# Taking out the matrix products that nobody reads in the gated recurrence of both layers

## The reference

```python
def hgrn_scan(k, v, log_f, s0, q=None):          # chunks of 64 tokens
    def step(s, inp):
        kc, vc, lf = inp[0], inp[1], inp[2]
        cum = jnp.cumsum(lf, axis=2)
        last = cum[:, :, -1:, :]
        s_new = jnp.exp(last[:, :, 0, :])[..., None] * s + \
            jnp.einsum('bhsd,bhse->bhde', kc * jnp.exp(last - cum), vc)
        ...
        decay = jnp.exp(jnp.where(mask, cum[:, :, :, None, :] - cum[:, :, None, :, :], -jnp.inf))
        att = jnp.einsum('bhtd,bhsd,bhtsd->bhts', qc, kc, decay)
        return s_new, o_inter + jnp.einsum('bhts,bhse->bhte', att, vc)
```

## Time and profile before

| | |
|---|---|
| median of 3 runs | 3832.34 us (3812.76, 3832.34, 3834.47) |
| the profiled execution's own time | 3829.4 us |
| its span in the trace | 3828.0 us |
| mean granted TensorE clock | 0.98 of full |
| busy: matmul, weight load | 3685.2 us (96%), 3061.2 us (80%) |
| busy: DVE, ACT, POOL | 1829.5 us (48%), 1188.7 us (31%), 159.9 us (4%) |
| transfers | 341 MB, mean 89 GB/s |
| recurrence of layer 0, layer 1 | about 417 to 504 us, 1418 to 1500 us |

### The profile page before, as it was taken

The page is one execution under the profiler, slowest core; times in us unless marked ns, Lnnn a source line. Parts: engine busy times, 40 slices in busy tenths (PEclk is TensorE's granted clock), DMA queues, the critical chain, the costliest instruction groups (busy, mean ns, idle before and its releaser), DMA issues.

```text
span 3828.0 us, 49948 instructions
## 1 busy us (share of the span) xinstructions
PE 3685.2 (96%) x21352; PEld 3061.2 (80%) x21352; DVE 1829.5 (48%) x2571; ACT 1188.7 (31%) x1621; POOL 159.9 (4%) x129
## 2 busy tenths in 40 slices
PE   7999899999999888999999999899999999999998
PEld 5866788888887567888888888588889888888887
DVE  4125764222244366533463457764446444656445
ACT  3115343111132262422342233442224222334222
POOL 0000310000000002000000001000000000010000
PEclk9999799999999998999999999999999999999999
DMA  6414011111111112222322222123222222222221
GB/s 255 151 62 153 15 45 56 67 63 59 67 67 70 58 57 78 99 99 98 112 99 99 99 100 78 45 75 113 99 89 98 101 98 99 100 89 100 99 95 59
DMA packets 51083, 341.26 MB, mean 89 GB/s; under 512 B 5760, under 2 KB 7968, under 8 KB 12720
## 3 DMA queue, kind: packets, MB, share of 16 engines
q1 hardware_dynamic: 43344, 301.09, 22.0%
q0 software_dynamic: 5216, 34.88, 2.4%
q10 hardware_dynamic: 2304, 2.10, 0.2%
HBM read 335.95 MB, written 2.10 MB: 88 GB/s over the span
## 4 chain that ended last, share of the span: by engine, by line
PE 88%; DVE 6%; ACT 2%; issue 2%; POOL 1%; DMA 1%; SPq 0%; DVEq 0%; ACTq 0%; POOLq 0%
PE PS L491 47%; PE PS L524 20%; PE PS L493 6%; PE PS L2231 2%; PE PS L1270 2%; PE PS L1286 1%; DVE nmax_a L1419 1%; PE PS L1325 1%; PE PS L1564 1%; PE PS L899 1%; PE PS L829 1%; PE PS L1857 1%; DVE WL L468 1%; ACT WH L463 1%; DVE SQ L734 0%
## 5 line engine op out<-in xcount | busy, mean ns | idle before, releaser
L468 DVE TENSOR_TENSOR WL<-raw,WH 128x2048 fp32r<-128x2048 f32 x260 | 595.6, 2292 | 306.3 <-ACT WH L463 306.3
L463 ACT ACTIVATE WH<-raw 128x2048 fp32r<-128x2048 f32 x260 | 495.0, 1906 | 543.2 <-PE PS L491 346.6
L491 PE MATMUL PS<-XH_ff,WL 128*128 128x512 f32 x640 | 253.5, 396 | 0.0
L491 PE MATMUL PS<-XH_ff,WH 128*128 128x512 f32 x640 | 251.9, 394 | 0.7 <-DVE GA_ff L2372 0.7
L491 PE MATMUL PS<-XL_ff,WH 128*128 128x512 f32 x640 | 250.9, 392 | 0.0
L2391 DVE TENSOR_TENSOR GA_ff<-PS,GA_ff 128x512 f32<-128x512 f32 (+1 forms) x63 | 36.0, 599 | 326.4 <-PE PS L493 219.1
L491 PE MATMUL PS<-XH_a,WH 128*128 128x512 f32 x448 | 174.3, 389 | 0.0
L491 PE MATMUL PS<-XL_a,WH 128*128 128x512 f32 x448 | 174.3, 389 | 0.0
L491 PE MATMUL PS<-XH_a,WL 128*128 128x512 f32 x448 | 174.3, 389 | 0.0
L491 PE MATMUL PS<-XH_b,WH 128*128 128x512 f32 x448 | 174.3, 389 | 0.0
L491 PE MATMUL PS<-XL_b,WH 128*128 128x512 f32 x448 | 174.3, 389 | 0.0
(11 more groups left out here) (463 smaller groups left out, 8990.9 us busy)
## 6 DMA issues: line engine op xcount, KB each, us to landing
raw<-in_panels SPq DMA_DIRECT2D x260, 1024.0 KB, 4.8
ada_win<-in_ada_panels POOLq DMA_DIRECT2D x18, 1024.0 KB, 5.1
ada_at<-in_ada_panels SPq DMA_DIRECT2D x12, 1024.0 KB, 4.8
piece<-in_ada_panels SPq DMA_DIRECT2D x24, 512.0 KB, 5.9
ada_start<-in_ada_panels POOLq DMA_DIRECT2D x6, 1024.0 KB, 18.1
FX<-in_dft_x POOLq DMA_DIRECT2D x2, 2048.0 KB, 8.1
X<-in_xT SPq DMA_DIRECT2D x4, 768.0 KB, 11.3
out<-X ACTq DMA_DIRECT2D x16, 128.0 KB, 1.7
```

The lines of the kernel that those rows point to most:

```text
L463: H.up(ac.activation(WH[s].rearrange("p k n -> p (k n)"), raw[:, n % 2, :], ACT.Copy), n)
L468: L.up(ve.tensor_tensor(WL[s].rearrange("p k n -> p (k n)"), raw[:, n % 2, :], WH[s].bitcast(F32).rearrange("p k n -> p (k n)"), ALU.subtr ...
L491: t = te.matmul(PS[:, j, :], lhsT, x[:, k, 0:SEQ], start=st, stop=end)
```

## The change

`dense` and its two calls are taken out, 9 matmuls in all: 2 in layer 0, and 2 and then 5 times 1 in layer 1. Nothing else is edited, in no other engine's code. Each call also waited for its bank; where a panel or a level goes into that bank next, it has that wait itself.

```diff
-            def dense(to, n):
-                wait_bank(to)
-                for _ in range(n):
-                    te.matmul(PS[:, to, :], BO, U[:, UQ, 0:SEQ], start=True, stop=True)
-
             def panel_parts(m, to):
                 wait_bank(to)
                 for q in (2 * m, 2 * m + 1):
@@
                 if g == 1:
                     for m in steps[-1]:
                         panel_parts(m, 4 + m)
-                    dense(3, 2)
             for u in range(UNITS):
                 level(u, panel_sums if l == 0 and u == 0 else None)
                 if l and u - 1 in steps:
                     panel_sums(steps[u - 1], 3, 0)
                 if l and u < 5:
-                    dense(7, 1)
                     for m in steps[u]:
                         panel_parts(m, 7)
```

## The result

| | before | after |
|---|---|---|
| median of 20 runs | 3825.22 us | 3835.60 us |
| lowest | 3812.76 us | 3814.53 us |
| profiled execution, own time | 3829.4 us | 3814.53 us |
| its span, mean granted clock | 3828.0 us, 0.98 | 3813.2 us, 0.98 |

The ratio of the two kernels is 1.0025, 95% interval 1.0013 to 1.0037: the change costs about 10 us. One of the 20 runs before took 8640 us; without it the median moves by 0.1 us. The changed kernel in a second comparison gave 1.0035 (1.0017 to 1.0053). I had forecast a gain of 3.5 us.

The account below looks back on a forecast made before the run. The prediction took TensorE, with 88% of the chain of waits, to bound the kernel. A gain of 5.0 us less a 1.5 us clock cost gave -3.5 us, from the 3832.3 us median a forecast of 3829 us, range 3812 to 3847.

Parts of the forecast that it names:

- What bounds the kernel: Whole kernel: TensorE holds 88% of the chain of waits, so work taken from its own stream is worth asking after.
- part 1, the prices on the path: Layer 1, five single dense products on the path: 5.76 us removed, less 0.7 us waiting for DVE, gain 5.0 us.
- the 0.7 us taken off for it: Layer 1, unit 5: waits 0.5 us for DVE's mask copies after unit 3, plus some 0.2 us of signalling.
- The pieces' transfers: Layer 1, pieces landing for the panel products: 0.6 us left to spare, so no cost, priced at 0 to 1 us.
- Part 2: Both layers, four products beside ACT's sigmoids: 0 us gained; earlier clock fall in layer 0 costs 1.5 us, at most 1.6.
- The clock in layer 1: Layer 1, around 1436 to 1437 us: without the dense product the clock rises at about the same time.
- rival 1 in full: Layer 1: clock stays at 1.2 GHz through the panels; 3844 us, or 3847 from the median; chance 0.15.
- in part: Layer 1: a later clock rise, or a fall in between, gives -3 to +10 us; chance 0.15.
- Rival 1's price: Layer 1, clock low until self products are done: 19.5 us lost less 5.76 us taken out, +13.8 us.
- Its point of decision: Layer 1: clock low for more than a quarter of the stage (5.0 / 19.5), and the gain is gone.
- Rivals 2 and 3: 2: DVE takes layer 1's gain, 3832 us, chance 0.10. 3: layer 0's clock fall unmoved, DVE loses nothing, 3826.5, chance 0.15.

Follow-up runs that it names:

- the run with the corner products: All nine dense products kept, same 512 columns, but through 32 rows by 32 columns, against the kernel before: 1.0050, 3838.26 beside 3819.02 us.
- five ahead, one between: Five dense products instead of two after the turned values in both layers, those between units kept, against the kernel before: 0.9980, 3814.11 beside 3819.02 us.
- five ahead, none between: Five dense products after the turned values in both layers, none between the units of layer 1, against the kernel before: 0.9983.
- five ahead, one at units 1 and 3: Five dense products after the turned values; between layer 1's units only those at units 1 and 3 stay, against the kernel before: 0.9965, 3815.99 beside 3829.18 us.
- ten in layer 0: Five dense products after the turned values, plus one ahead of each group of units 1 to 5 of layer 0, against the kernel before: 1.0021.
- eleven in layer 0: Five dense products after the turned values, ten among layer 0's units 1 to 5, one ahead of unit 0's second group, against the kernel before: 1.0017.

## Why the prediction was wrong

**What bounds the kernel** and **part 1, the prices on the path**, held: the five are worth their 5.76 us where the clock is up. The 5.0 us that came of them was met by luck (4.8 in the first trace): DVE did not hold unit 5, so the 0.7 us taken off for it was wrong, and 0.9 us went to a panel at 1.2 GHz that the sum did not have. From the end of the first sums those mask copies moved ahead by 2.4 us (23.8 to 21.4), where I had 1.92 as the limit. The pieces' transfers held nobody.

**Part 2** was right in kind and too large: without the two products layer 0 took 87.8 to 88.3 us in four traces, and 86.3 to 87.5 in the three that have them as before, so about 1 us more and not 1.5, with a scatter of the same size. In the first trace the self products do start 1.65 us later behind the first transpose (46.96 against 45.31 us), but they take 4.53 us in place of 5.36, since the clock rises earlier in them. "In layer 1 ... nothing is left to lose" was probably wrong in effect: with the two gone as well as the five the loss is 12.5 us, with the five alone gone 4.6 us (0.0012 of 3821). The intervals overlap, and the reported clocks, 0.975 and 0.977, speak for a difference. By which steps the two help the later clock is not settled; the two traces of these kernels both show it lost. What the runs do show is the converse, that more products in the same place raise the clock of the stage (0.92 in its first 64 us against 0.83).

**The clock in layer 1** is the step that failed. I argued that it would rise at about the same time, because a panel product had preceded the rise, and went from the rise straight to a gain that is kept; I put nothing in the sum for a clock that falls again. The rise did come so in both traces of the changed kernel. The hold did not: in one it fell again for units 2, 4 and 5 and the stage took 8.4 us more than before, and with layer 1 alone changed it never rose before the self products, 13.1 us more.

The traces also show behind what it falls. Once the units of layer 1 were under way, with or without dense products, it fell nine times in six of the 13 traces, each time within 0.5 us after the end of a level and eight sum records at 2.4 GHz, some 3 us of narrow work (units 0, 1, 3 and 5), and never behind a level with four sum records (units 2 and 4). It did not fall each time: in the first trace of the changed kernel it held behind units 1, 3 and 5. And where no dense product stood ahead of the panels, each rise came within the second panel of a pair or as it ended; but not each pair brought one, and no single panel did. The one dense product a unit stood just where the fall comes; why it holds the clock there in most of the cases is argued from this and not shown.

I had both rows against it on the table, the 40 us of levels at 0.50 in layer 0 and the fall at 1471, and weighed them for the rise only. One of them was read too strongly: over the 40 us of layer 0 TensorE was not busy 1.00 but 36.3 of 41.0 us, idle for 2.2 us twice, waiting for DVE. With 0.15 on rival 1 in full and 0.15 in part, I gave 0.30 to what, by the clocks that the runs report, happened in most executions.

**Rival 1's price** held: +13.8 us forecast up to the end of the self products, where the trace with the clock low throughout has +13.8 (60.0 against 46.2 us from the first transpose), and +13.1 for the whole stage (94.2 against 81.1 us). Its place held too. Its point of decision, a quarter of the stage at 1.2 GHz, no run tried by itself. The trace with the clock back for two of the five units is at +8.4.

**Rivals 2 and 3** did not occur: levels did not wait on `att` in every unit, and the fall in layer 0 did move: from 9.4 us behind the first transposes to 6.0 in the first trace after and 8.1 in the second.

**The numbers.** The range and "within 1%" held the time (3835.6; 1.0025), the sign did not: faster was forecast and slower measured. The base was off too: the three runs shown had a median 7 us above that of the 20, and by that luck the 3829 us lie nearer to the measured time than their sum would. The Trainium skill's advice, "TensorE: Matmul & The Clock Gate", section "Why this matters for your kernels", to keep TensorE busy without longer gaps, came out on the right side; the run with the corner products shows that keeping it busy is not the whole of it.

## What to carry to other kernels

A product whose result nobody reads may be there for the clock: price its removal at both levels of the clock for everything around it, and ask not only whether the clock will rise without it but whether it will hold. Where TensorE idles behind another engine and narrow products follow, filling the idle stretch is free and kept the clock up here (0.9980); dense products among the units of layer 0, a stage that waits for other engines, cost more than they returned (1.0017, 1.0021). And one trace of a kernel whose clock falls and rises is one draw: the fastest of twenty runs was the one that was traced.

## What the runs showed of the hardware

- A TensorE without an idle moment can sit at 1.2 GHz for 46.8 us (the row of layer 0 above, levels with ten dense products between them), and 512 columns through a corner of 32 x 32 did not do what the same columns through the whole array did: 97.7 against 81.1 us for the stage, at the same 1.9 us a product at 1.2 GHz.
- The same code with the same inputs has the clock at different places from one execution to the next. The changed kernel spread from 3814.5 to 3846.9 us in 20 runs, with its reported clock from 0.980 to 0.971.
- The same large products ran at one of two paces, at a granted clock of 1.00 in both. In the feed-forward part between the two recurrences, which no kernel here edits, TensorE was busy all the time, and 400 us hold 2266 records in the first row, of the kernel before, and 2309 in the second, of the changed one:

```profile
700.00:1100.00 400.00, 400.00 (x2266) 346.83 (x2265) 107.59 (x109) 72.82 (x74) 0.00 (x0) 1.00 0.18 64
...
700.00:1100.00 400.00, 400.00 (x2309) 352.72 (x2308) 112.25 (x115) 74.97 (x78) 0.00 (x0) 1.00 0.18 64
```

All 13 traces have one of these two paces, five the slower. The 1.9% between them hold over some 600 us, so by my estimate they are worth 11 us, as much as the whole effect measured here, and 11 of the 15 us by which the first trace after is shorter than the one before; the stretch is only 8 us shorter, since the clock was lower in it in the changed kernel's trace (0.98 against 0.99). What it comes from was not tried. How often each kernel runs at either pace is not known, so the sizes of the effects in the medians may hold some of it; that the clock in layer 1 is lost does not rest on it, since the lower reported clocks and the lengths of the stages show that by themselves. The lengths in the traces, in us:

| kernel | layer 0 | between | layer 1 | pace |
|---|---|---|---|---|
| before | 87.5 | 913.9 | 81.1 | slower |
| changed, first and second trace | 88.3, 87.8 | 905.8, 902.3 | 76.1, 89.5 | faster |
| only the five out | 86.3 | 901.0 | 90.8 | faster |
| only the two out, both layers | 88.3 | 905.9 | 80.2 | faster |
| only the two of layer 0 out | 87.8 | 905.2 | 80.3 | faster |
| changed in layer 1 alone | 87.5 | 899.5 | 94.2 | faster |
| corner of the array | 88.3 | 912.1 | 97.7 | slower |
| five ahead, one between | 84.4 | 899.6 | 76.2 | faster |
| five ahead, none between | 84.4 | 913.9 | 72.8 | slower |
| five ahead, one at units 1 and 3 | 86.0 | 913.9 | 76.2 | slower |
| ten in layer 0 | 101.1 | 903.6 | 77.8 | faster |
| eleven in layer 0 | 95.3 | 912.2 | 76.2 | slower |
